# Experts' rows by indirect DMA instead of one-hot matmuls, with twelve weight buffers

## What is computed

```python
h2 = rmsnorm(x, norm2_g) * (1.0 + scale2) + shift2
logits = h2 @ router_w + router_b ; probs = softmax(logits)     # 16 experts in 4 groups
g = argmax(sum of the top-2 probs of each group); experts = top-2 inside g, weights normalised
hidden = silu(h2 @ w_gate[e]) * (h2 @ w_up[e])                  # 1024 -> 512, for the tokens of e
y = sum over e of combine[:, e] * (hidden @ w_down[e])          # 512 -> 1024
x = x + gate2 * y
```

## Time and profile before

| | us |
|---|---|
| median of 3 runs | 861.25 (860.85 to 864.91) |
| profiled execution | 861.29 |
| its span | 859.6 |
| PE busy | 801.4 (93%) |
| DVE busy | 612.0 (71%) |
| ACT busy | 479.9 (56%) |
| POOL busy | 74.3 (9%) |

### The profile page before, as it was taken

The page is one execution under the profiler, slowest core; times in us unless marked ns, Lnnn a source line. Parts: engine busy times, 40 slices in busy tenths (PEclk is TensorE's granted clock), DMA queues, the critical chain, the costliest instruction groups (busy, mean ns, idle before and its releaser), DMA issues.

```text
span 859.6 us, 10823 instructions
## 1 busy us (share of the span) xinstructions
PE 801.4 (93%) x4010; PEld 633.8 (74%) x4012; DVE 612.0 (71%) x820; ACT 479.9 (56%) x618; POOL 74.3 (9%) x67
## 2 busy tenths in 40 slices
PE   3799999999999889999999679999999999999993
PEld 2687787776666556678888568888888888888872
DVE  4686887425998875535763658788888888888881
ACT  6334224455656345555234446868686868686850
POOL 4020000000000000010000000111111111111111
PEclk9799999999999999999999889999999999999997
DMA  9919993111031111152261519698989898989863
GB/s 275 341 33 371 389 370 143 50 50 50 1 99 49 50 50 50 50 172 98 98 245 50 199 54 330 240 351 295 349 294 347 296 348 298 345 296 351 293 224 52
DMA packets 83995, 172.87 MB, mean 201 GB/s; under 512 B 7744, under 2 KB 27304, under 8 KB 81904
## 3 DMA queue, kind: packets, MB, share of 16 engines
q1 hardware_dynamic: 79200, 156.29, 50.7%
q0 software_dynamic: 4752, 16.03, 7.8%
HBM read 161.78 MB, written 10.52 MB: 200 GB/s over the span
## 4 chain that ended last, share of the span: by engine, by line
PE 82%; DVE 7%; ACT 4%; DMA 3%; issue 2%; SPq 1%; POOL 0%; POOLq 0%; DVEq 0%; ACTq 0%
PE ps L615 20%; PE ps L617 19%; PE ps L616 19%; PE ps L1021 7%; PE ps L771 4%; DMA raw<-in_w_in 1%; PE ps L753 1%; PE ps L855 1%; DVE w_lo L1507 1%; PE ps L871 1%; PE ps L883 1%; DMA raw<-in_w_ada 1%; DVE accm L1566 1%; PE ps L786 1%; ACT w_hi L1137 1%
## 5 line engine op out<-in xcount | busy, mean ns | idle before, releaser
L1830 DVE TENSOR_TENSOR w_lo<-raw,w_hi 128x2048 fp32r<-128x2048 f32 x96 | 215.6, 2286 | 16.8 <-ACT w_hi L1402 16.8
L1402 ACT ACTIVATE w_hi<-raw 128x2048 fp32r<-128x2048 f32 x96 | 180.0, 1909 | 11.3 <-PE ps L617 11.3
L615 PE MATMUL ps<-act_lo,w_hi 128*128 128x512 f32 x232 | 98.7, 426 | 6.9 <-DVE act_lo L1549 2.8
L615 PE MATMUL ps<-w_lo,hgT_hi 128*128 128x512 f32 x256 | 102.2, 399 | 2.5 <-DVE w_lo L1830 2.5
L617 PE MATMUL ps<-w_hi,hgT_hi 128*128 128x512 f32 x256 | 100.5, 393 | 0.0
L616 PE MATMUL ps<-w_hi,hgT_lo 128*128 128x512 f32 x256 | 100.4, 392 | 0.0
L617 PE MATMUL ps<-act_hi,w_hi 128*128 128x512 f32 x232 | 91.4, 394 | 0.0
L616 PE MATMUL ps<-act_hi,w_lo 128*128 128x512 f32 x232 | 91.3, 394 | 0.0
L1137 ACT ACTIVATE w_hi<-raw 128x2048 fp32r<-128x2048 f32 (+2 forms) x29 | 51.9, 1793 | 68.0 <-DMA raw<-in_w_in 44.9
L1507 DVE TENSOR_TENSOR w_lo<-raw,w_hi 128x2048 fp32r<-128x2048 f32 (+2 forms) x29 | 61.9, 2145 | 32.1 <-ACT w_hi L1137 32.0
L594 POOL DMA_INDIRECT out<-ys,slot_tok x16 | 49.3, 3084 | 314.8 <-DVE ys L1938 314.8
(11 more groups left out here) (265 smaller groups left out, 1514.1 us busy)
## 6 DMA issues: line engine op xcount, KB each, us to landing
raw<-in_w_gate SPq DMA_DIRECT2D x32, 1024.0 KB, 8.8
raw<-in_w_up SPq DMA_DIRECT2D x32, 1024.0 KB, 6.8
raw<-in_w_down SPq DMA_DIRECT2D x32, 1024.0 KB, 8.6
raw<-in_w_in SPq DMA_DIRECT2D x16, 1024.0 KB, 6.5
raw<-in_w_ada SPq DMA_DIRECT2D x16, 1024.0 KB, 7.3
raw<-in_w_ada SPq DMA_DIRECT2D x8, 512.0 KB, 7.0
raw_early<-in_w_ada SPq DMA_DIRECT2D x8, 512.0 KB, 5.1
raw<-in_w_out SPq DMA_DIRECT2D x4, 1024.0 KB, 5.0
```

What stands on the lines that cost most here:

```text
L615: pe.matmul(o, a[0], b[1], start=start, stop=False)
L1402: act.activation(e_hi[s_][:, :], e_raw[r][:, :], ACT.Copy).then_inc(e_top, 1)
L1830: dve.tensor_tensor(e_lo[s_][:, :], e_raw[r][:, :], e_hi[s_][:, :].bitcast(F32), ALU.subtract).then_inc(e_split, 1)
```

## The change

The normalised rows are no longer kept in SBUF as two halves. ACT writes them unsplit into `hn` (`rows_scaled`), POOL stores them in DRAM (`rows_d`, four tiles of 0.5 MB). For each expert POOL then issues an indirect DMA (`fetch`) that reads the rows of its slots into `gx`, by the token numbers of `slot_index`. TensorE transposes them (`turn_rows`: 16 transposes of 128 x 128 for a pair, four a unit) where the gather stood. `hgT_hi`, `hm`, `hgT_lo` are made as before.

So that the token numbers are there earlier, `pick`, `slot_table` and `slot_index` of a pair run one pair ahead, in stage b = 0: `pick(X + 2)` after the first split, `slot_table(X + 2)` after `turn_hid(X)`, `slot_index(X + 2)` after `hidT_lo`. For the first pair they run before the first rows are fetched. On POOL the order in a pair is scatter, fetch, fetch, scatter.

The memory that comes free holds twelve raw buffers (SP's wait is for chunk z - 12). There is one result buffer `ys` where there were two: `scaled(X)` waits for all scatters before X. `hid` is written over `silu`. The low halves of the rows (`rows_low`, four instructions of DVE) go away; the slot table is made during routing.

```diff
-E_RAW = 6
+E_RAW = 12
...
+    rows_d = nc.dram_tensor("rows_scratch", [S, D], F32, kind="Internal").ap()
...
-    h2_hi = at("h2_hi", [NT, D], F32R, 128)
-    h2_lo = at("h2_lo", [NT, D], F32R, 182)
+    hn = at("hn", [NT, D], F32, 128)
...
     hgT_hi = at("hgT_hi", [2, KD, P], F32R, 144)
     hgT_lo = at("hgT_lo", [2, KD, P], F32R, 152)
-    ys = [at(f"ys{i}", [D], F32, 160 + 4 * i) for i in range(2)]
-    sel = at("sel", [NT, 2, P], F32R, 168)
-    silu = at("silu", [F_EXP], F32, 98)
-    hm = [at(f"hm{i}", [2, 2, P], F32, 101 + 2 * i) for i in range(2)]
-    hid = at("hid", [F_EXP], F32, 178)
+    hm = at("hm", [2, KD, P], F32, 152)
+    ys = at("ys", [D], F32, 160)
+    gx = [at(f"gx{i}", [D], F32, 164 + 4 * i) for i in range(2)]
+    sel = [at(f"sel{i}", [NT, P], F32R, (200, 172)[i]) for i in range(2)]
+    silu = at("silu", [F_EXP], F32, 178)
...
+    e_raw = [at(f"raw_late{i}", [CH], F32, 182 + 8 * i) for i in range(2)] + [raw[2], raw[3], raw[0], raw[1]] + [
+        at(f"raw{i}", [CH], F32, kb) for i, kb in ((4, 80), (5, 88), (6, 96), (7, 104), (8, 128), (9, 136))]
     e_hi = [w_hi[1], w_hi[2], w_hi[0], at("w_hi3", [CH], F32R, 112)]
...
 
-            def stage_loads(X, e, z0, first_):
-
+            def stage_loads(X, e, b, first_):
+
+                z0 = 0 if first_ else 10 - 6 * b
                 for cc in range(4 if first_ else 6):
                     r = (z0 + cc) % E_RAW
                     z = EC * X + cc - (0 if first_ else 2)
-                    if not first_ or not isinstance(X, int):
-                        sp.wait_ge(e_split, z - E_RAW + 1) if not isinstance(z, int) or z >= E_RAW else None
-                    if isinstance(z, int) and z < E_RAW:
-                        if z < 2:
-                            sp.wait_ge(m_sp, KD)
-                        elif z < 4:
-                            sp.wait_ge(chunk_split, N_RAW - 3 + z)
-                        else:
-                            sp.wait_ge(seg_ready, seg_done("wo1", 3))
+                    if not isinstance(z, int) or z >= E_RAW:
+                        sp.wait_ge(e_split, z - E_RAW + 1)
+                    elif z < 2:
+                        sp.wait_ge(ob_ps, 2 * NT)
+                    elif z < 4:
+                        sp.wait_ge(m_sp, KD)
+                    elif z < 6:
+                        sp.wait_ge(chunk_split, N_RAW - 5 + z)
+                    elif z < 10:
+                        sp.wait_ge(seg_ready, seg_done("wo1", 3))
+                    else:
+                        sp.wait_ge(st_rows, 16 * NT)
                     if cc < 4:
...
+                pool.wait_ge(h2_rows, tt + 1)
+                pool.dma_start(rows_d.rearrange("(t p) d -> p t d", p=P)[:, tt], hn[:, tt]).then_inc(st_rows, 16)
...
                     pool.wait_ge(scat, 16 * X)
-                pool.indirect_dma_start(out[0], bass.IndirectOffsetOnAxis(slot_tok[:, X % 2:X % 2 + 1], 0),
-                                        ys[X % 2][:, :], None, compute_op=ALU.add).then_inc(scat, 16)
-
-            for X in range(N_EXP):
-                scatter(X)
+                pool.indirect_dma_start(out[0], bass.IndirectOffsetOnAxis(slot_tok[:, X % N_EXP:X % N_EXP + 1], 0),
+                                        ys[:, :], None, compute_op=ALU.add).then_inc(scat, 16)
+
+            def fetch(X):
+
+                pool.wait_ge(idx_ok, X - X % 2 + 2)
+                if X >= 2:
+                    pool.wait_ge(hg_ps, 2 * (X - X % 2))
+                pool.indirect_dma_start(gx[X % 2][:, :], None, rows_d,
+                                        bass.IndirectOffsetOnAxis(slot_tok[:, X % N_EXP:X % N_EXP + 1], 0)
+                                        ).then_inc(rows_in, 16)
+
+            def expert_pass(X0):
+                fetch(X0)
+                fetch(X0 + 1)
+                for X in range(X0, X0 + N_EXP, 2):
+                    if X > X0:
+                        scatter(X - 2)
+                    if X + 2 < X0 + N_EXP:
+                        fetch(X + 2)
+                        fetch(X + 3)
+                    if X > X0:
+                        scatter(X - 1)
+                scatter(X0 + N_EXP - 2)
+                scatter(X0 + N_EXP - 1)
+
+            pool.wait_ge(st_rows, 16 * NT)
...
 
-            def gather(X, units):
+            def turn_rows(X, units):
 
 
                 for u in units:
                     if u == 0:
-                        pe.wait_ge(sel_ready, X + 2)
+                        pe.wait_ge(rows_in, 16 * X + 32)
                     if not isinstance(X, int) or X > 0 or u >= 2:
                         pe.wait_ge(hg_sp, 2 * X + u - 1)
-                    for kk in (2 * u, 2 * u + 1):
-                        for tt in range(NT):
-                            for n, part in enumerate((h2_hi, h2_lo)):
-                                last = pe.matmul(ps[2 + u % 2][:, 2 * P * (kk % 2):2 * P * (kk % 2) + 2 * P],
-                                                 part[:, tt, P * kk:P * kk + P], sel[:, tt, :, :],
-                                                 start=(tt == 0 and n == 0), stop=(tt == NT - 1 and n == 1))
+                    for j in range(2):
+                        kk = 2 * u + j
+                        for b in range(2):
+                            last = pe.transpose(ps[2 + u % 2][:, P * (2 * j + b):P * (2 * j + b) + P],
+                                                gx[b][:, P * kk:P * kk + P], ident[:, :])
                     last.then_inc(hg_ps, 1)
 
...
 
+                pe.wait_ge(sel_ready, X + 2)
...
+                    t = pe.transpose(ps[4][:, P * f:P * f + P], silu[:, P * f:P * f + P], ident[:, :])
                 t.then_inc(hidT_ps, 1)
...
                 turn_hid(X)
-                if b == 0:
-                    slot_table(X, e)
+                if b == 0 and more_:
+                    slot_table(X + 2, e + 2)
 
             def expert_pass(X0):
-                gather(X0, range(4))
+                slot_table(X0, 0)
+                turn_rows(X0, range(4))
                 stage(X0, 0, 0, True, False)
                 stage(X0 + 1, 1, 1, False, False)
...
-                act.activation(h2_hi[:, tt, :], xres[:, tt, :], ACT.Copy, scale=st[:, tt, 5:6]).then_inc(h2_hiR, 1)
+                act.activation(hn[:, tt, :], xres[:, tt, :], ACT.Copy, scale=st[:, tt, 5:6]).then_inc(h2_rows, 1)
 
             def high_e(z, zi, turn):
...
                 act.activation(silu[:, :], ps[0][:, :], ACT.Silu).then_inc(silu_ok, 1)
                 if not first_:
-                    high_e(z + 5, z0 + 5, X + 1)
...
                                       ).then_inc(sel_ready, 1)
 
-            def slot_index(X, b):
-
-                dve.wait_ge(ws_ps, X - b + 2)
-                if not isinstance(X, int) or X >= 2:
-                    dve.wait_ge(scat, 16 * (X - 1))
-                dve.tensor_copy(slot_tok[:, b:b + 1], ps[7][:, 4 * b:4 * b + 1])
-                dve.tensor_reduce(slot_w[:, b:b + 1], ps[7][:, 4 * b + 1:4 * b + 3], AX.X, ALU.add).then_inc(idx_ok, 1)
-
-            def scaled(X, b, last_=False):
+            def slot_index(X, e, again):
+
+                dve.wait_ge(ws_ps, X + 2)
+                if again:
+                    dve.wait_ge(scat, 16 * (X - N_EXP + 2))
+                found = ps[7][:, 0:8].rearrange("p (b n) -> p b n", n=4)
+                dve.tensor_copy(slot_tok[:, bass.ds(e, 2)].unsqueeze(2), found[:, :, 0:1])
+                dve.tensor_reduce(slot_w[:, bass.ds(e, 2)], found[:, :, 1:3], AX.X, ALU.add).then_inc(idx_ok, 2)
...
+            def scaled(X, e, b, last_=False):
 
                 dve.wait_ge(e_used, EC * X + (6 if last_ else 10))
-                if not isinstance(X, int) or X >= 2:
-                    dve.wait_ge(scat, 16 * (X - 1))
-                dve.wait_ge(idx_ok, X + 1)
+                if not isinstance(X, int) or X >= 1:
+                    dve.wait_ge(scat, 16 * X)
                 for n in range(2):
-                    dve.scalar_tensor_tensor(out=ys[b][:, 512 * n:512 * n + 512], in0=ps[5 + n][:, :],
-                                             scalar=slot_w[:, b:b + 1], in1=gate2[:, 512 * n:512 * n + 512],
+                    dve.scalar_tensor_tensor(out=ys[:, 512 * n:512 * n + 512], in0=ps[5 + n][:, :],
...
+                if b == 0 and more_:
+                    slot_index(X + 2, e + 2, again)
                 if not last_ and not turn:
                     low_e(nz + 2, nz0 + 2)
-                slot_index(X, b)
...
+                slot_index(X0, 0, again)
+                if again:
                     for cc in range(3):
                         low_e(EC * X0 + cc, cc)
+                else:
+                    low_e(1, 1)
...
```

More of the change, by code:

```diff
@@ L601, in _ @@
             with pool.If(more > 0):
-                for X in range(N_EXP, PASSES * N_EXP):
-                    scatter(X)
+                for p in range(1, PASSES):
+                    expert_pass(p * N_EXP)
                 pool.wait_ge(scat, 16 * PASSES * N_EXP)
```

(7 more changed lines are left out.)

149 lines of the change are left out of this document (70 added, 79 removed).

## The result

The changed kernel takes 857.03 us (median of nine runs; 852.0 to 860.04) against 862.97 for the kernel before in the same runs: a ratio of 0.992 with an interval of 0.989 to 0.995. Run again beside other kernels, it gave 853.62 us and 0.991 [0.989, 0.994]. It is faster by 0.8 to 0.9%, where I forecast 870.7 us and slower: the sign was wrong. The profiled execution took 856.1 us, its span is 854.4.

What follows compares the result with a forecast made beforehand. TensorE sets the period, DVE and DMA close behind; without the gather, rows through DRAM give 42.7 us. 859.6 + 7.7 (start) + 2.5 (seven periods) - 0.8 (last pair) = 869.0 span, forecast 870.7 us; eight in ten 849 to 885.

Steps and rivals of the forecast that it cites:

- PE's work: TensorE's work per expert pair: the gather's 7.7 us leaves, 1.8 us of transposes comes in, 36.4 us remains.
- Chain 1: Fetched rows through ACT's and DVE's splits to the second up chunk: PE stands 2.4 to 2.6 us, period floor 39.0.
- S: The moment PE starts turn_rows, from which the path is counted; forecast at 510.6 us for the first pair.
- The clock: After the stall before the second up chunk, TensorE's clock falls to 0.50 for 3.4 us, lifting the floor to 40.6.
- Chain 2: Rows through DRAM, from turn_hid via slot_index and two fetches to turn_rows: period 32.9 us plus landing, 42.7 in all.
- the spacing of the fetches: On GpSimd, the first fetch holds POOL 3.34 us, so the second starts 5.6 us after turn_hid.
- the landing L: Time from the second fetch's start until its rows land: 9.8 us taken, bounds 5.4 to 11.4.
- second sum: Landing of the second fetch summed by DMA packets: 6.8 + 2.9 + 0.5 = 10.2 us.
- rival A: Rows land early, within 7.0 us or less: period 40.6, span 852.3, time 854 us; chance 0.28.
- Start: Ahead of the experts, the first turn_hid comes at 530.9 us, 7.7 us later than before.
- Edits at nothing: Dropped rows_low, twelve raw buffers with earlier loads, one ys, and silu shared with hid: no gain or loss.
- Rival D: DMA becomes the bound as fetches cost 3.6 us or more and the lead runs out: up to 10 us; chance 0.05.

Runs made afterwards that it cites:

- e2_fill: Changed kernel plus 18 identity transposes per pair on TensorE, before the wait for the second half of the row splits; 849.99 us, ratio 0.985 to the kernel before.
- e5_space20: Changed kernel plus twenty short chained memsets on GpSimd between the two fetches of a pair; 898.14 us, ratio 1.042 to the kernel before.
- e4_space: Changed kernel plus seven short chained memsets on GpSimd between the two fetches of a pair; 857.07 us, ratio 0.996 to the kernel before.
- e3_lead6: Changed kernel with twelve raw buffers, each load held until the split six chunks before it is done; 851.68 us, ratio 0.989 to the kernel before.
- e8_lead6_again: Changed kernel with loads held to a lead of six chunks, repeated beside the changed kernel; 852.20 us, ratio 0.991 to the kernel before.
- e1_stale: Changed kernel without the fetches of all pairs but the first, later pairs reusing the first pair's rows; 848.07 us, ratio 0.985 to the kernel before.
- e7_early: Changed kernel with the next pair's slot table and index moved ahead of the even expert's down products; 855.31 us, ratio 0.996 to the kernel before.
- v7_order: Changed kernel with one weight split moved behind row splits on ScalarE and VectorE; 854.97 us, ratio 0.994 to the kernel before.
- v5_six_start: Changed kernel with six raw and six split buffers, early index, VectorE's split order kept, identity transposes in the start; 850.55 us, ratio 0.989 to the kernel before.

## Why the prediction was wrong

- **PE's work**: right. 36.4 forecast, 36.6 measured.
- **Chain 1**: right. The chunk starts 12.7 us after S (12.9 forecast), PE stands in front of it 2.1 us (2.4 to 2.6), and the floor of the period is 38.7 (39.0), shown by the periods without a clock drop and by e2_fill.
- **The clock**: right in size, 1.6 us a period; wrong in that I gave it to every pair. It came in six of seven pairs of one execution of the changed kernel and in four of the other.
- **Chain 2, its form**: right. The first fetch starts 2.2 us after `turn_hid`; the 27.3 us from the landing to the next mark held to 0.7 us in e5_space20.
- **Chain 2, the spacing of the fetches: the step that failed.** I took 3.34 us of GpSimd for the first fetch, from scatters that run beside splits. It takes 1.01. The row was the wrong one for the place: a scatter starts amid splits, while the first fetch starts behind `slot_index`, where VectorE has just ended small instructions and the next split is 0.7 us away. I had the price of 1.54 us for an idle VectorE in the same rows, and what VectorE does at that moment in the timeline, and did not put them together. That is 2.1 of the 3.5 us by which the rows came earlier than I had them. It is not the distance between the two starts as such: e4_space has the 3.4 us of the forecast between them and periods of 40.5 to 40.7, since the second fetch then starts behind the split and is not held. What I had done was to charge VectorE's hold to both fetches, 3.34 us for the first and 1.6 us within L for the second; the kernel pays it once.
- **Chain 2, the landing L**: 8.4 us where I took 9.8, in my bounds (5.4 to 11.4), 1.4 us too long. In the pair of 614.49 the second fetch's first packet moves 5.7 us after its start (6.8 in my second sum, from a scatter held 3.34 us and not 2.53), the last 2.3 us later (2.9), and the landing follows after 0.4 (0.5). By spacing and landing the rows are there 11.9 us after the mark and not 15.4, and PE comes to them at 12.1: they are hidden, chain 1 governs, and the period is that of rival A, 40.6. A's condition, L below 7.8, was worked out with the wrong spacing; the same sum with the right one gives L below 9.8 (40.6 - 27.3 - 3.5), and the 8.4 meets it. So the spacing alone turns the forecast of 42.7 into 40.6 (27.3 + 3.5 + 9.8), the landing alone only into 41.3 (27.3 + 5.6 + 8.4). A's number came, not its reason: beside loads the first packet still comes 3.0 us after GpSimd is done with the fetch (618.50 after 615.50), and 0.6 us after it where the queues are idle (the scatter of 840.4). The Trainium skill, "SBUF — State Buffer", box on DVE and SWDGE, says that GpSimd can't write descriptors while DVE, in a mode that takes both ports, keeps it out of the shared port pair. I had cited it for the size alone; read as a matter of time it would have given the right spacing. The traces show a hold of the same kind for a TENSOR_TENSOR with both inputs in SBUF, an instruction that the box doesn't name: a fetch that starts 0.7 us ahead of one takes 1.01 us, and one that starts inside it ends 0.9 us behind it (617.48, 618.33).
- **Start**: +5.6 us against +7.7; S came at 507.9 and not 510.6, mostly by the same two terms (the first fetch held for 2.23 us, a landing of 7.5 us against 9.0); from S to the mark it is 20.9 us against 20.3.
- **Edits at nothing**: right, the lead by e3_lead6 and e8_lead6_again; one `ys` and the shared `silu` show no wait of DVE or ACT for them in the changed kernel. Rival D did not appear, although the DMA engines are as good as full (share 1.01 to 1.04).
- **The last pair**: I had 0.8 us less; the tail is 0.9 us longer.

In numbers: the seven periods changed by -11.7 us where my sum has +2.5, 14.2 below it, the start came 2.1 below, the tail 1.7 above, and 869.0 - 14.2 - 2.1 + 1.7 is the span of 854.4. (The +2.5 is itself a slip: seven times 42.7 less 42.29 is 2.9.) Rival A had 852.3 for the span, at a chance of 0.28. What I should have seen is that its condition hung on two terms and not on L alone, both with a lower end in the rows.

What is shown: that the fetch is hidden (e1_stale, e7_early), how near it is (e4_space, e5_space20), that the longer lead of the loads brings nothing (e8_lead6_again), and what the clock costs (e2_fill). That chain 1 sets 38.7 us is shown by its stall in all pairs; but shortening it alone (v7_order) brought nothing, so the limit of the stretch seems to be as much the sum of ScalarE's and VectorE's work. An order that reaches PE's 36.4 us was not found.

## What to carry to other kernels

Price an instruction by what the other engines do at the moment when it starts, not by the median of its kind: a gather issued on GpSimd cost 1.0 us when it started ahead of a split of VectorE and 2.5 us when it started inside one (a scatter 1.5 us beside an idle VectorE and 3.4 inside a split), and with that the forecast turned. Where a new chain runs beside an old one, work out when each arrives at the point where they meet (here 11.9 against 12.1 us), and give each term of the difference its own two ends. And where TensorE has a stall of 2 us that can't be removed, dummy transposes in it and in the start were worth more here (0.977 against 0.992, each to the kernel before measured beside it) than the change itself; where there is no stall they cost their time.

## What the runs showed of the hardware that I had not expected

- GpSimd's time for an indirect DMA depends on where in VectorE's work it starts. A gather of 128 rows of 4 KB holds GpSimd 0.93 to 1.01 us when it starts ahead of a TENSOR_TENSOR that reads and writes SBUF alone, or in the same moment (531.93 in the changed kernel), or beside VectorE instructions that read PSUM (617.76 in e4_space). When it starts inside such a TENSOR_TENSOR it ends 0.8 to 0.9 us behind it. In the worst case (v5_six_start) a scatter got no turn between six such instructions and took 11.2 us. Why it slips in between two of them elsewhere (3.39 us in the changed kernel) stays open.
- Landing of such a gather in the two executions of the changed kernel, DMA queues full: a pair's first fetch, which nothing held, 5.8 to 7.3 us after its start, of which about 1 is GpSimd's time; the second, held and 1.3 us behind the first, 8.2 to 10.4.
- The granted clock fell to 0.50 (1.2 GHz) for 3.4 us after some stalls of 2.1 us and not after others of the same length in the same kernel (six of seven, four of seven), for 6.8 us at each of the seven stalls of 5.9 to 7.4 us in e5_space20, and never after the fourteen stalls of 1.0 to 1.2 us in seven pairs of v7_order. Stretches that differ only in this differ by 1.6 us, so that single periods of one execution can't be compared without looking at the clock.
